# The down projection of a gated FFN as seven block products with the block sums made on the fly

## What is computed

```
def conv_gated_ffn(h, w_up, conv_w, w_down):
    up = causal_depthwise_conv(h @ w_up, conv_w)
    gate, val = jnp.split(up, 2, axis=-1)
    return (jax.nn.silu(gate) * val) @ w_down
...
        h = rms_norm(x, ffn_norm_g[l])
        x = x + conv_gated_ffn(h, w_up[l], ffn_conv_w[l], w_down[l])
```

## Time and profile before

| | |
|---|---|
| median of three runs | 1596.8 us |
| the profiled execution | 1598.57 us |
| its span | 1596.8 us |
| PE busy | 1502.4 us, 94% |
| DVE busy | 927.5 us, 58% |
| ACT busy | 640.5 us, 40% |
| POOL busy | 126.6 us, 8% |
| moved by DMA | 153.67 MB, 96 GB/s over the span |

### The profile page before, as it was taken

The page is one execution under the profiler, slowest core; times in us unless marked ns, Lnnn a source line. Parts: engine busy times, 40 slices in busy tenths (PEclk is TensorE's granted clock), DMA queues, the critical chain, the costliest instruction groups (busy, mean ns, idle before and its releaser), DMA issues. The chain is left out here.

```text
span 1596.8 us, 19266 instructions
## 1 busy us (share of the span) xinstructions
PE 1502.4 (94%) x7254; PEld 1260.8 (79%) x7254; DVE 927.5 (58%) x1329; ACT 640.5 (40%) x1065; POOL 126.6 (8%) x104
## 2 busy tenths in 40 slices
PE   5999999998999988998999879999999999999999
PEld 4899977776877776885787767888888888888887
DVE  4321255664675666765854468888878777334334
ACT  4331225554424553124532235555555555332232
POOL 2000040000420003111200000000000000000000
PEclk9899999999999999999999979999999999999999
DMA  5111131103121002325661202322222223544643
GB/s 199 44 57 52 57 99 34 46 28 124 34 81 46 30 27 68 86 66 188 213 231 66 67 27 79 101 85 79 80 90 83 79 79 106 191 151 159 230 151 132
DMA packets 126502, 153.67 MB, mean 96 GB/s; under 512 B 11530, under 2 KB 94397, under 8 KB 126141
## 3 DMA queue, kind: packets, MB, share of 16 engines
q1 hardware_dynamic: 126224, 152.40, 29.1%
q10 hardware_dynamic: 189, 0.08, 0.0%
HBM read 115.55 MB, written 36.31 MB: 95 GB/s over the span
## 5 line engine op out<-in xcount | busy, mean ns | idle before, releaser
L1838 PE MATMUL ps<-split_arena 128*128 128x512 f32 x1320 | 309.4, 391 | 3.3 <-DVE split_arena L2376 2.5
L516 PE MATMUL ps<-split_arena 128*128 128x512 f32 x1152 | 290.3, 404 | 10.7 <-ACT plain_arena L551 4.9
L1838 PEld LDWEIGHTS ps<-split_arena 128*128 128x128 f32 x1320 | 248.7, 189 | 56.1 <-DVE split_arena L2376 3.1
L516 PEld LDWEIGHTS ps<-split_arena 128*128 128x128 f32 x1152 | 214.7, 192 | 56.1 <-issue 10.4
L1901 DVE TENSOR_TENSOR down_a<-plain_arena,down_a 128x1024 fp32r<-128x1024 f32 x44 | 53.9, 1224 | 143.4 <-ACT down_a L1890 143.4
L1928 PE MATMUL ps<-down_w,down_a 128*128 128x512 f32 x352 | 137.0, 389 | 0.0
L1930 PE MATMUL ps<-down_w,down_a 128*128 128x512 f32 x352 | 137.0, 389 | 0.0
L1929 PE MATMUL ps<-down_w,down_a 128*128 128x512 f32 x352 | 136.9, 389 | 0.0
L1838 PE MATMUL ps<-up_b,split_arena 128*128 128x512 f32 x528 | 129.9, 396 | 4.9 <-DVE split_arena L1766 4.9
L1838 PEld LDWEIGHTS ps<-up_b,split_arena 128*128 128x128 f32 x528 | 101.5, 192 | 26.6 <-DVE split_arena L1766 5.2
L1890 ACT ACTIVATE down_a<-plain_arena 128x1024 fp32r<-128x1024 f32 x44 | 46.7, 1061 | 159.6 <-PE ps L1930 137.3
(11 more groups left out here) (345 smaller groups left out, 2478.8 us busy)
## 6 DMA issues: line engine op xcount, KB each, us to landing
plain_arena<-scr_act SPq DMA_DIRECT2D x44, 512.0 KB, 3.6
plain_arena<-in_w_in SPq DMA_DIRECT2D x24, 512.0 KB, 4.1
scr_gate<-plain_arena SPq DMA_DIRECT2D x48, 256.0 KB, 2.0
plain_arena<-scr_gate SPq DMA_DIRECT2D x24, 512.0 KB, 3.9
plain_arena<-in_w_up SPq DMA_DIRECT2D x22, 512.0 KB, 5.2
up_raw<-in_w_up SPq DMA_DIRECT2D x22, 512.0 KB, 5.0
scr_act<-plain_arena SPq DMA_DIRECT2D x22, 512.0 KB, 2.7
plain_arena<-in_w_down SPq DMA_DIRECT2D x44, 256.0 KB, 3.8
```

Source lines behind the costliest of these rows:

```text
L516: mm = nc.tensor.matmul(m.ps[:, self.banks[half], :], w[:, k, :], src[:, k, h * BANK:(h + 1) * BANK], start=(j == 0), stop=(j == self.PER_ ...
L1838: mm = nc.tensor.matmul(o, self.w[j][w][:, k, :], self.h[j][k][h], start=(j in self.OPENS and k == 0 and n == 0), stop=(k == self.HK - 1 a ...
```

## The change

The diff, cut to its core:

```diff
-    ORDER = (6, 7, 0, 1, 3, 4, 5, 2)
-    FT = FF // P
-    STEPS = 2 * FT
+    ORDER = (2, 1, 7, 6, 4, 5, 3)
+    HF = FF // P // 2
+    STEPS = 7 * HF
+    CHUNKS = (HF + 1) // 2
+    OPENS = (2, 1, 7, 3)
+    SLOTS = 4
...
+        for what, first, per, count in (("s3", 19, 2, C), ("t3", 20, 2, C), ("t2", 28, 2, C), ("s2", 29, 2, C), ("t4", 41, 1, HF),
+                                        ("s1", 50, 2, C), ("t1", 51, 2, C), ("s4", 63, 1, HF)):
...
+    def step_of_use(self, u):
+        return self.step_of((2, 4, 3)[u // self.HF], u % self.HF)
...
+    def load_slot(self, sp, u):
+        HF, S = self.HF, self.SLOTS
+        k, which = u % HF, u // HF
+        if u >= S:
+            sp.wait_ge(self.lo, self.step_of_use(u - S) + 1)
+        f, s = HF + k, u % S * BANK
+        if which in (0, 2):
...
+            sp.dma_start(self.all[:, self.a_slot + s:self.a_slot + s + BANK], self.m.scr_act[f][:, 0:BANK]).then_inc(self.slot_in[u % S], 16)
+        if which in (0, 1):
+            sp.dma_start(self.all[:, self.b_slot + s:self.b_slot + s + BANK],
+                         self.m.ins["w_down"][0, f * P:(f + 1) * P, 0:BANK]).then_inc(self.slot_in[u % S], 16)
...
+    def split_hi(self, act, n):
+        j, k = self.ORDER[n // self.HF], n % self.HF
+        c = k // 2
+        if n >= 3:
+            act.wait_ge(self.mm, n - 2)
+        if j == 2:
+            act.wait_ge(self.slot_in[self.use(n) % self.SLOTS], self.slot_full(self.use(n)))
...
+    def split_lo(self, dve, n):
+        dve.wait_ge(self.hi, n + 1)
...
+        else:
+            j, at, name = {"t4": (4, self.b_slot, "b11"), "s4": (3, self.a_slot, "a11")}[what]
+            u = self.use(self.step_of(j, c))
+            dve.wait_ge(self.slot_in[u % self.SLOTS], self.slot_full(u))
+            dve.wait_ge(self.summed, self.made["t2" if what == "t4" else "s2", c // 2])
...
+            ins = V.tensor_tensor(slot, slot, self.all[:, other:other + BANK], ALU.subtract)
...
                 if i == LAST:
-                    for s in range(2):
-                        down.load(sp, s)
+                    sp.wait_ge(up.mm[2], LAST + 1)
+                    for u in range(down.SLOTS):
+                        down.load_slot(sp, u)
                 up.store(sp, i - 1)
-            down.load(sp, 2)
-            down.load(sp, 3)
+            sp.wait_ge(up.mm[7], LAST + 1)
+            down.load_first(sp, 0), down.load_first(sp, 1)
+            sp.wait_ge(up.mm[4], LAST + 1)
+            down.load_first(sp, 2)
+            for c in range(3, 6):
+                down.load_slot(sp, c + 1)
+                down.load_first(sp, c)
             up.store(sp, LAST)
...
+            down.load_x(sp, 0)
+            sp.wait_ge(up.mm[3], LAST + 1)
+            for c in range(4):
+                down.load_slot(sp, c + 7)
+                down.load_second(sp, c)
...
+            for n in range(4, down.STEPS):
+                for what, c in down.sums_at(n):
+                    down.sum(dve, what, c)
+                down.split_lo(dve, n)
+                if n in (16, 53):
+                    down.add_x_to_copy(dve, 2 if n == 16 else 7)
+                if n == 24:
+                    down.add_p1(dve)
+                if n == 46:
+                    down.add_x_to_p6(dve)
+                if n == 57:
+                    down.add_p4(dve)
+                if n == 68:
+                    down.add_p5(dve)
```

More of the change, by code:

```diff
@@ L1844 @@
 class DownProjection:
-    ORDER = (6, 7, 0, 1, 3, 4, 5, 2)
-    FT = FF // P
-    STEPS = 2 * FT
+    ORDER = (2, 1, 7, 6, 4, 5, 3)
+    HF = FF // P // 2
+    STEPS = 7 * HF
+    CHUNKS = (HF + 1) // 2
+    BANKS = {j: (2, 3, 4, 5) if j in (1, 6, 5) else (6, 7, 0, 1) for j in range(1, 8)}
+    OPENS = (2, 1, 7, 3)
+    SLOTS = 4
+    F0 = RW
     def __init__(self, m, up, row_trips):
         self.m, self.up = m, up
[L1854 to L1925, removed]
-            cut = slice(t * P, (t + 1) * P)
[L1927 to L1930, removed]
@@ new lines, in __init__, with sums_at @@
+        self.x_in, self.res_in = row_trips[0], row_trips[2:2 + self.CHUNKS]
+        self.slot_in = [m.sem(f"down_slot_in{i}") for i in range(self.SLOTS)]
+        self.hi, self.lo, self.mm, self.summed, self.copied, self.added, self.last, self.saved = (
+            m.sem(f"down_{n}") for n in ("hi", "lo", "mm", "summed", "copied", "added", "last", "saved"))
+        order = [x for n in range(self.STEPS) for x in self.sums_at(n)]
+        self.made = {x: n + 1 for n, x in enumerate(order)}
+    def sums_at(self, n):
+        HF, C = self.HF, self.CHUNKS
+        out = []
+        for what, first, per, count in (("s3", 19, 2, C), ("t3", 20, 2, C), ("t2", 28, 2, C), ("s2", 29, 2, C), ("t4", 41, 1, HF),
+                                        ("s1", 50, 2, C), ("t1", 51, 2, C), ("s4", 63, 1, HF)):
+            c, r = divmod(n - first, per)
+            if r == 0 and 0 <= c < count:
+                out.append((what, c))
+        return out
@@ new lines, in _ @@
+            sp.wait_ge(up.c21, LAST + 1)
+            sp.wait_ge(up.c22, LAST + 1)
+            for c in range(6):
+                down.load_third(sp, c)
+            for u in range(11, 15):
+                down.load_slot(sp, u)
+            down.load_x(sp, 1)
+            down.write_out(sp, 0)
+            for u in range(15, 18):
+                down.load_slot(sp, u)
+            down.load_x(sp, 2)
+            for u in range(18, 24):
+                down.load_slot(sp, u)
+            down.load_x(sp, 3)
@@ L2142, in _ @@
+            down.load_slot(sp, 24), down.load_slot(sp, 25)
+            down.write_out(sp, 1)
+            for u in range(26, 29):
+                down.load_slot(sp, u)
+            down.write_out(sp, 2)
+            for u in range(29, 33):
+                down.load_slot(sp, u)
+            for t in range(4):
+                down.write_last(sp, t)
+            sp.wait_ge(down.saved, 7 * 16)
         @block.scalar
@@ L2521, in _ @@
             up.product(pe, 3, LAST)
-            for s in range(down.STEPS):
-                down.step(pe, s)
+            for n in range(down.STEPS):
+                down.step(pe, n)
 def hybrid_trunk(nc, ins):
```

211 lines of the change are left out of this document (183 added, 28 removed).

## The result

| | median | lowest to highest | runs |
|---|---|---|---|
| before | 1597.28 us | 1595.27 to 1603.64 | 6 |
| after | 1607.95 us | 1606.2 to 1611.55 | 6 |

The ratio after / before is 1.0061, with a 95% interval of 1.0038 to 1.0084. The change made the kernel 10.7 us slower; 132 matmuls fewer did not pay. The forecast was 1608 us.

A forecast was written before the change was run, and what follows sets the result against it. PE was taken to bound the last third. -29.9 + 11.9 + 13.8 + 1.5 + 12.9 + 0.7 = +10.9 us, so a median of 1608 us from 1596.8; 8-in-10 range 1597 to 1622.

The forecast's parts named there:

- The saving: Down projection: 924 matmuls in place of 1056, 132 x 0.2263 = 29.9 us less on PE.
- The rings: Two seven-step groups: DVE split, load, sum, next split in turn; period 4.73 us against PE's 2.72.
- T4's ring: Steps 45 to 51: slots released by the split directly ahead of the sum; PE waits 13.8 us.
- S4's: Seven late periods, sums from n = 67, slots released by the split directly ahead; PE waits 12.9 us.
- P3's ring: The same wait as S4's: seven periods, 33.1 us, and four DVE passes after n = 68; cost 12.9 us.
- The burst: Steps 7 to 10: first loads share one queue at 385 GB/s, slots land late; PE waits 11.9 us.
- 15.5 MB: Bytes through SP's queue, from the store of block 20, before slot use 10 has landed; 2.72 us per MB.
- The lead and the cover: Three operand buffers give splits 2.9 us of lead; with DVE's overlapped passes, steps 11 to 43 cost nothing.
- The 1.5 us that I gave P5: Sums S1 and T1 meet the sums after n = 53 and 57, DVE starting late; about 1.5 us.
- fixed part: Time of a transfer besides its bytes in the queue, about 2.1 us, used to place use 10's landing.
- The clock: PE's granted clock may fall in gaps, a step then taking up to 5.4 us; 0.7 us for all.
- half clock in the rings: Rival, chance 0.12: every ring step at the lower clock, 0.7 us more in each of 14 steps; 1618 us.

The follow-up runs named there:

- both: Kernel after, with slot uses 4 to 10 loaded ahead of residual and later chunks, and sums T4 and S4 two steps later; 1569.34 us, ratio 0.9809.
- doubled loads: Kernel after, with slot uses 11 to 21 each also loading a 256 KB block of A into the slot's other half; 1624.84 us, one run.
- slots first: Kernel after, with slot uses 4 to 10 loaded ahead of the residual read and all chunks of A21, B12, B22; 1594.55 us, ratio 0.9988.
- residual behind: Kernel after, with only the 1 MB residual read moved, from ahead of slot use 7 to behind use 10; 1607.1 us, ratio 1.0064.
- The run with a step less: The kernel with both cures, with the split of step n waiting for PE's step n-2 in place of n-3; 1586.98 us, one run.
- sums one later: Kernel after, with sums T4 and S4 one step later in DVE's list (first at 42 and 64); 1586.92 us, ratio 0.9923.

## Why the prediction was right, and where it was off

**The saving.** 924 matmuls at 0.2266 us. Kernel "both" shows it nearly bare: 27.1 us in medians, 29.9 less a lag of 2.0 by the ledger.

**The rings.** Right in place, number and form: gaps at steps 45 to 51 and 67 to 73 and nowhere between, all released by the split L2012, which had been behind a landing. The period was forecast at 4.73 us; it is 4.64 in P6, where the loads read `w_down`, and about 4.5 in P3, where they read `scr_act` and land in 2.5 to 2.6 us for a forecast of 2.8. T4's ring cost 14.9 for 13.8, S4's 14.9 for 12.9. In S4's one wait was 4.71 us in place of 2.65:

```profile
1579.69 0.69 DVE L2046 TENSOR_TENSOR down_all<-down_all 128x512 f32<-128x512 f32 x1 [2.68 <-DMA down_all<-scr_act]
1580.30 1.22 DVE L2012 TENSOR_TENSOR down_ops<-down_all,down_ops 128x1024 fp32r<-128x1024 f32 x1
1586.23 0.69 DVE L2046 TENSOR_TENSOR down_all<-down_all 128x512 f32<-128x512 f32 x1 [4.71 <-DMA down_all<-scr_act]
```

The queue was nearly empty then (0.02 of share from 1585 to 1587). This load, of use 32, is the last load of the kernel, and it is the slow one of P3's ring in each of the four traces that have this ring: 4.66 us from issue to landing here, 4.47 with the doubled loads, 3.30 in "slots first", 3.18 in "residual behind", where the six others took 2.5 to 2.8. So it is no single accident. What makes it slow stays open. PE's first matmul behind it in this trace:

```profile
1588.11 0.60 PE L2118 MATMUL ps<-down_ops 128*128 128x512 f32 x1 [3.52 <-DVE down_ops L2012]
```

and in "residual behind", whose lists are the same at this place:

```profile
1590.44 0.50 PE L2118 MATMUL ps<-down_ops 128*128 128x512 f32 x1 [2.04 <-DVE down_ops L2012]
```

There P3's ring cost 11.9 us and not 14.9: the gap was 1.5 us shorter, and step 73 took 2.89 us and not the 4.45 of half clock. So the forecast's 12.9 was 1.0 too high for the ring alone, and a late landing (1.5 us) and the clock behind it (1.6) made it 14.9.

**The burst.** Nearly the right steps, and the right growth: from step 7 on 2.7 to 3.0 us a step. But steps 5 and 6 were already 1.0 and 2.2 us late, where the forecast had nothing before step 7, and the size was 2.7 us too low, 14.6 for 11.9. The rate was right: 390 GB/s for my 385 (the first window of after). What failed is the term "15.5 MB", the bytes that go through the queue before use 10 has landed. SP issued its second half at 1375.71, and it landed 10.33 us later:

```profile
1375.66 0.05 issue
1375.71 10.33 DMA down_all<-in_w_down
```

By the forecast's own formula, from the first store at 1339.14 (SP's timeline), it would have landed at 1339.14 + 2.1 + 15.5 x 2.70 = 1383.1, at 388 GB/s; it landed at 1386.0. Most of the 2.9 us was there from the start: use 4 (4.0 MB by the same count) landed at 1354.9 where the formula gives 1352.0, use 7 at 1369.5 for 1366.9. Two windows, up to the store and from it to the landing, tell what moved:

```profile
1333.00:1339.14 6.14, 6.14 (x29) 5.07 (x27) 5.64 (x6) 2.00 (x4) 0.00 (x0) 1.00 0.67 195
1339.14:1386.04 46.90, 37.85 (x151) 29.22 (x150) 19.45 (x17) 15.05 (x16) 0.00 (x0) 0.94 1.05 387
```

The queue was not empty when the store was issued. The eight loads of uses 0 to 3, 2 MB, had been issued from 1333.44 on, and at 195 GB/s 1.1 MB of them had moved: 0.9 MB were still ahead of the store, and the 15.5 MB leave them out. From the store to the landing 387 GB/s make 17.3 MB (MB of 1024 KB, as before), which is 0.9 MB more than 15.5 + 0.9. So some transfers issued behind use 10 had moved before it was complete. Against these 1.8 MB stands the formula's fixed part of 2.1 us, in which the full queue moves 0.8 MB; the 1.0 MB left are the 2.7 to 2.9 us. That the 16 DMA engines are not in step would let later transfers pass; no run tests it.

**The lead and the cover.** 2.9 us, and nothing lost in steps 11 to 44, with DVE at 50 of 60 us. The run with a step less confirms it with 14.7 us for an expected 13. The 1.5 us that I gave P5 are 0.0 in after and 1.5 and 1.4 in the runs "slots first" and "sums one later". In after PE was slow in step 51, the last of the ring (next point), which gives DVE 1.6 us to catch up; "residual behind" and the doubled loads have the same slow step 51 and no lag in P5 either. That this is the cause is argued and not tested alone.

**The clock.** The forecast's 0.7 us is its second mis-sized term: it is 3.2 us. In after the granted clock fell to its 1.2 GHz level for three of the rings' gaps, of 2.63, 3.25 and 3.52 us, and stayed at 2.4 GHz behind the others, of 0.4 to 2.2 and of 2.84 us. Two stretches of T4's ring, behind gaps of 1.61 and of 2.63 us, and one at the end of S4's, behind 3.52:

```profile
1492.00:1496.00 4.00, 3.02 (x12) 2.17 (x12) 0.61 (x2) 0.78 (x1) 0.00 (x0) 1.00 0.74 286
...
1513.00:1517.00 4.00, 3.54 (x9) 2.82 (x10) 4.00 (x5) 0.00 (x0) 0.00 (x0) 0.57 0.30 80
...
1588.00:1592.00 4.00, 3.89 (x10) 3.08 (x11) 2.33 (x3) 0.00 (x0) 0.00 (x0) 0.57 0.00 0
```

Inside a ring a slow step costs little, since PE would have waited. At the end, as the forecast said, it is not given back: step 51 took 4.34 us for 2.72, 1.6 us of T4's 14.9, and step 73 took 4.45, of which "residual behind", at full clock, shows 1.6 to be the clock's. Without it T4's ring is 13.3; in the run "slots first", whose step 51 took 2.83 us, it is 13.1, for a forecast of 13.8. The rival "half clock in the rings", in every step, did not come true. The Trainium skill, "TensorE: Matmul & The Clock Gate", section "HAM oscillation — how this bites in real kernels", tells of a kernel whose short bursts of matmuls are parted by transfer waits of about 3 to 5 us, and whose clock falls each time. The trace agrees for gaps over 3 us: it fell behind both of the rings' and behind the one of 3.52 us in P2. But it fell behind shorter ones too: behind 2.63 us in T4's ring, behind 2.41 us in P2 (before step 9), and in "slots first" behind 2.17 us before step 73, where one of 2.24 us before step 48 had left it alone. So the length of the gap alone does not decide.

**The hit of the median** is better than its parts, and so in part luck. The parts were 3.6 us too low together (40.8 for 44.4): the burst by 2.7, the clock by 2.5 and the late last landing by 1.5, against 1.5 us too much for the rings and 1.5 too much for P5. And the unchanged first 1340 us vary by more than that from run to run.

## What to carry to other kernels

A buffer must be released several steps ahead of the instruction that waits for its next content, counted in the list of the engine that does both; where the release is the instruction directly ahead of the wait, every step costs a whole round trip of a transfer, however idle the queue is. In one queue, what is needed next must be issued first: large loads for later belong behind the small ones for now. And before work is taken from the bound engine, work out the lead of what feeds it; here one step of lead was worth 15 us, and the order of two lists 40.

## What the runs showed of the hardware

- In the rings of after, a 256 KB load from a queue with nothing else in it landed 2.66 to 2.85 us after its issue when it read `w_down`, and 2.47 to 2.64 us when it read `scr_act`. One behind the residual read took 3.34, and the last of the kernel 4.66. In the run with doubled loads two of them, issued 0.4 us apart, took 0.8 us longer together. A 1 MB write landed in 4.2 us.
- With 2 KB rows one queue held 386 to 397 GB/s (windows of 6 us) for over 40 us while PE, DVE and ACT were reading and writing the same memory, and the 128x1024 split kept its 1.22 to 1.23 us in it.
- Transfers issued into the full queue between 1349 and 1394 us landed 8 to 13 us later. Before use 10 had landed, about 0.9 MB more had moved than had been issued up to it.
